# TensorE takes every other conditioning tile of the first quarter, with the raw tile standing and the vector's column moving

## What is computed

```python
cond = jax.nn.silu(c)                     # (1, 2048)
mod = cond @ w_ada[l] + b_ada[l]          # w_ada: 2048 x (9 * 2048) f32
sh1, sc1, gt1, sh2, sc2, gt2, sh3, sc3, gt3 = jnp.split(mod, N_MOD, axis=-1)
h = modulate(rmsnorm(x, g_ffn1_pre[l]), sh1, sc1)     # h * (1 + sc1) + sh1
y = rmsnorm(swiglu(h, w1_gate[l], w1_up[l], w1_down[l]), g_ffn1_post[l])
```

## Time and profile before

| | us |
|---|---|
| median of 3 runs (lowest, highest) | 1944.65 (1941.50, 1946.92) |
| the profiled execution | 1944.92 |
| its span, first to last instruction | 1943.1 |
| PE busy | 1862.8 (96%) |
| DVE busy | 1364.9 (70%) |
| ACT busy | 896.8 (46%) |

### The profile page before, as it was taken

The page is one execution under the profiler, slowest core; times in us unless marked ns, Lnnn a source line. Parts: engine busy times, 40 slices in busy tenths (PEclk is TensorE's granted clock), DMA queues, the critical chain, the costliest instruction groups (busy, mean ns, idle before and its releaser), DMA issues.

```text
span 1943.1 us, 24172 instructions
## 1 busy us (share of the span) xinstructions
PE 1862.8 (96%) x8522; PEld 1530.4 (79%) x8522; DVE 1364.9 (70%) x1667; ACT 896.8 (46%) x1138; POOL 0.2 (0%) x4
## 2 busy tenths in 40 slices
PE   3999999999999999799999997999999999999998
PEld 3788888888877778587887786888888888788886
DVE  6986877777778878879886796877654545544444
ACT  4677644444434433544445546444444444434443
POOL 0000000000000000000000000000000000000000
PEclk9999999999999999899999998999999999999999
DMA  9996888888878988678993494888766666566663
GB/s 372 391 385 215 268 273 270 282 289 278 287 263 309 359 298 306 226 248 283 306 307 115 137 335 136 274 288 279 251 190 189 190 188 192 167 193 195 194 195 131
DMA packets 254926, 488.26 MB, mean 251 GB/s; under 512 B 17414, under 2 KB 19836, under 8 KB 254588
## 3 DMA queue, kind: packets, MB, share of 16 engines
q1 hardware_dynamic: 253968, 486.66, 75.4%
q10 hardware_dynamic: 876, 0.53, 0.1%
HBM read 485.04 MB, written 2.10 MB: 251 GB/s over the span
## 4 chain that ended last, share of the span: by engine, by line
PE 83%; DVE 8%; DMA 3%; DVEq 3%; ACT 2%; issue 1%; SPq 0%; ACTq 0%
PE pair L1337 27%; PE pair L1339 26%; PE pair L1338 26%; DVE acc L856 2%; DMA raw<-in_w_down 2%; PE tps L1377 2%; DVE w_lo L837 2%; DVE start_acc L869 1%; DVEq L845 1%; DMA start_raw<-in_w_ada 1%; ACT w_hi L497 1%; PE mps L1421 1%; PE tps L1428 1%; PE mps L1404 0%; DVEq L868 0%
## 5 line engine op out<-in xcount | busy, mean ns | idle before, releaser
L497 ACT ACTIVATE w_hi<-raw 128x1024 fp32r<-128x1024 f32 x634 | 668.0, 1056 | 904.4 <-PE pair L1339 491.8
L837 DVE TENSOR_TENSOR w_lo<-raw,w_hi 128x1024 fp32r<-128x1024 f32 x634 | 769.8, 1218 | 427.0 <-ACT w_hi L497 423.2
L1337 PE MATMUL pair<-w_hi,h_hi 128*128 128x512 f32 (+1 forms) x1792 | 703.4, 393 | 10.2 <-DVE w_lo L837 8.8
L1339 PE MATMUL pair<-w_hi,h_lo 128*128 128x512 f32 (+1 forms) x1792 | 696.4, 389 | 0.0
L1338 PE MATMUL pair<-w_lo,h_hi 128*128 128x512 f32 (+1 forms) x1792 | 695.8, 388 | 0.0
L1337 PEld LDWEIGHTS pair<-w_hi,h_hi 128*128 128x128 f32 x1792 | 336.9, 188 | 83.6 <-DVE w_lo L837 6.9
L1339 PEld LDWEIGHTS pair<-w_hi,h_lo 128*128 128x128 f32 x1792 | 336.8, 188 | 69.9
L1338 PEld LDWEIGHTS pair<-w_lo,h_hi 128*128 128x128 f32 x1792 | 337.1, 188 | 66.8 <-issue 0.2
L856 DVE SCALAR_TENSOR_TENSOR acc<-raw,c_col,acc 128x512 f32<-128x512 f32 x420 | 315.6, 751 | 45.9 <-DMA raw<-in_w_ada 11.9
L1337 PE MATMUL pair<-w_hi,hid_hi 128*128 128x512 f32 x704 | 277.3, 394 | 5.7 <-DVE w_lo L837 5.7
L1339 PE MATMUL pair<-w_hi,hid_lo 128*128 128x512 f32 x704 | 274.3, 390 | 0.0
(11 more groups left out here) (161 smaller groups left out, 683.9 us busy)
## 6 DMA issues: line engine op xcount, KB each, us to landing
raw<-in_w_ada SPq DMA_DIRECT2D x224, 512.0 KB, 4.8
raw<-in_w_gate SPq DMA_DIRECT2D x176, 512.0 KB, 3.9
raw<-in_w_up SPq DMA_DIRECT2D x176, 512.0 KB, 4.1
raw<-in_w_down SPq DMA_DIRECT2D x176, 512.0 KB, 4.3
start_raw<-in_w_ada SPq DMA_DIRECT2D x64, 512.0 KB, 8.8
raw<-in_w_in SPq DMA_DIRECT2D x56, 512.0 KB, 4.6
raw<-in_w_o SPq DMA_DIRECT2D x32, 512.0 KB, 5.2
raw<-in_w_uq SPq DMA_DIRECT2D x6, 512.0 KB, 4.6
```

Of the source, the lines that this page charges most:

```text
L497: nc.scalar.activation(w_hi[:, w % HI_RING, :, 0:n], raw[:, r % RING, :, 0:n], ACT.Copy).then_inc(hi_ready, 1)
L837: nc.vector.tensor_tensor(w_lo[:, r % RING, :, 0:n], raw[:, r % RING, :, 0:n], w_hi[:, w % HI_RING, :, 0:n], ALU.subtract).then_inc(raw_us ...
L1337: nc.tensor.matmul(o, hi, wh, start=first and kk == 0, stop=False, skip_group_check=added)
L1339: ins = nc.tensor.matmul(o, lo, wh, start=False, stop=last and kk == 1, skip_group_check=added)
```

## The change

TensorE computes the products of the odd tiles of the first quarter (BY_PE) itself. start_turn(n) takes the raw tile as it landed: each of its 8 pieces of 128 columns is the standing operand, column j of silu(c) the moving one, and the products accumulate in the same 8 columns of mps into which start_columns(0) then adds the sums of VectorE's eight even tiles. start_turned counts these, and load_start waits for it where the tile whose buffer it reuses was TensorE's; start_used now counts VectorE's tiles only. On TensorE's queue tiles 1 and 3 stand ahead of the transposes of the columns, 5 to 11 behind them, both turns of x ahead of tile 13, then 13, 15 and start_columns(0). keep_warm(16) and the wait ahead of it are gone; keep_warm(20) stays. On VectorE the small works move to the places n = 6, 10 and 12. Later quarters are as before.

```diff
--- before.py
+++ after.py
@@ -60,6 +60,8 @@
 RING = 8
 HI_RING = 4
 START_RING = 7
+
+BY_PE = tuple(range(1, KD, 2))
 
 
 OPEN = 8
@@ -308,6 +310,7 @@
         restored = sem("restored")
         start_landed = [sem(f"start_landed{i}") for i in range(START_RING)]
         start_used = sem("start_used")
+        start_turned = sem("start_turned")
         start_sum = sem("start_sum")
         forget_landed = sem("forget_landed")
         rot_ready = sem("rot_ready")
@@ -362,6 +365,10 @@
                 if w < b.w_end:
                     return b, w - b.w
 
+        def by_dve(n):
+
+            return n - sum(k < n for k in BY_PE)
+
         def partial(v):
 
             return part[v % OPEN // OPEN_FF][:, v % OPEN_FF]
@@ -418,7 +425,11 @@
 
                 e, j = divmod(n, KD)
                 if n >= START_RING:
-                    sp.wait_ge(start_used, n - START_RING + 1)
+                    before = n - START_RING
+                    if before in BY_PE:
+                        sp.wait_ge(start_turned, BY_PE.index(before) + 1)
+                    else:
+                        sp.wait_ge(start_used, by_dve(before + 1))
                 sp.dma_start(start_raw[:, n % START_RING],
                              both[:, j, 0:2, e * NB:(e + 1) * NB]).then_inc(start_landed[n % START_RING], 16)
 
@@ -1053,11 +1064,13 @@
                 dve.wait_ge(setup, 1)
 
             for n in range(KD):
-                if n == 5:
+                if n in BY_PE:
+                    continue
+                if n == 6:
                     small_tiles()
-                if n == 9:
+                if n == 10:
                     power(N_X0, D, 2)
-                if n == 10:
+                if n == 12:
                     refine(N_X0)
                 start_ada(n)
 
@@ -1394,16 +1407,27 @@
                 for k in range(2):
                     transposes(n + k, [s[:, t, c * P:(c + 1) * P] for c in (2 * k, 2 * k + 1) for t in range(TT)], free)
 
+            def start_tile(tile, j, first, last):
+
+                for k in range(2 * DB):
+                    c = slice((k % 4) * P, (k % 4 + 1) * P)
+
+                    ins = nc.tensor.matmul(mps[:, 0, k:k + 1], tile[:, k // 4, c],
+                                           ones[:, 0:1] if j is None else c_col[:, 1, j:j + 1],
+                                           start=first and k == 0, stop=last, skip_group_check=True)
+                return ins
+
             def start_columns(e):
 
-                pe.wait_ge(start_used, KD * (e + 1))
+                pe.wait_ge(start_used, by_dve(KD * (e + 1)))
                 if e:
                     pe.wait_ge(gain_ready, e)
-                for k in range(2 * DB):
-                    c = slice((k % 4) * P, (k % 4 + 1) * P)
-                    ins = nc.tensor.matmul(mps[:, 0, k:k + 1], start_acc[:, e % 2, k // 4, c], ones[:, 0:1],
-                                           start=True, stop=True)
-                ins.then_inc(start_sum, 1)
+                start_tile(start_acc[:, e % 2], None, e > 0, True).then_inc(start_sum, 1)
+
+            def start_turn(n):
+
+                pe.wait_ge(start_landed[n % START_RING], 16 * (n // START_RING + 1))
+                start_tile(start_raw[:, n % START_RING], n, n == BY_PE[0], False).then_inc(start_turned, 1)
 
             def keep_warm(n):
 
@@ -1442,17 +1466,21 @@
                         after()
 
 
+            pe.wait_ge(c_ready, 1)
+            start_turn(1)
+            start_turn(3)
             pe.wait_ge(small_landed, SMALL)
             nc.tensor.transpose(mps[:, 1, 0:P], y[:, 0, 0:P], ident)
             rest = V_ROWS - P
             nc.tensor.transpose(mps[:, 1, P:V_ROWS], y[0:rest, 0, P:2 * P], cst[0:rest, 0:rest]).then_inc(cols_full, 1)
-            turn_x(tp["mod1"], XN["ffn1"], 0)
+            for n in BY_PE[2:]:
+                if n == 13:
+                    turn_x(tp["mod1"], XN["ffn1"], 0)
+                    turn_x(tp["mod1"], XN["ffn1"], 1)
+                start_turn(n)
+            start_columns(0)
 
             pe.wait_ge(setup, 1)
-            pe.wait_ge(start_used, KD - 3)
-            keep_warm(16)
-            start_columns(0)
-            turn_x(tp["mod1"], XN["ffn1"], 1)
             keep_warm(20)
 
             for v in range(4 * OPEN):
```

## The result

The changed kernel is slower: a median of 1951.81 us (9 runs, 1949.57 to 1953.75) against 1944.0 (9 runs, 1939.42 to 1948.83), a ratio of 1.0040 with an interval of 1.0032 to 1.0049, which is 7.8 us (6.2 to 9.5). Its profiled span is 1950.4 us, 7.3 more than before.

What follows compares the result with a forecast made beforehand. TensorE, busy 96%, bounds the kernel; what counts is when start_columns(0) ends: 38.76 becomes 44.9 (+6.1), taken as +6.4 on 1944.92, giving 1951.3, or 1951.0 for the median. Range 1945.5 to 1955.

Steps and rivals of the forecast that it cites:

- The price of a tile: TensorE's 16 one-column instructions per odd tile: 3.44 us at the low clock, against 2.57 us for two arrivals.
- The timetable: TensorE's opening: tiles 5 to 11 done at 32.7, turns 34.4, tiles 13 and 15 41.3, columns' end 44.9: +6.1 us.
- the waits ahead of the groups: Possible waits before TensorE's seven groups: 3.58 instead of 3.44 us each would make +7.1; +6.4 was taken.
- the mark: Not a forecast term: start of the second start_columns, at 80.64 in the kernel before, used to compare traces.
- The early part: Tiles 1 and 3 and column transposes on TensorE until about 14.5, hidden before 18.9; uncovered, it would cost 0.5 us.
- The clock: TensorE's opening: one-column matmuls don't lift the low 1.2 GHz clock, so groups stay at 3.44 us.
- rival A: Clock rises early under unbroken TensorE work, later tiles take 1.7 us: -3.5 us, 1941.2; chance 0.12.
- rival B: Clock rises at the turns of x; tiles 13, 15 and the columns take 1.7 us: +1.2 us, 1945.9; chance 0.06.
- Rival C: First weight products start at the low clock, +2.4 us after slack: +8.8 us in all, 1953.7; chance 0.12.
- Transfers: SyncE's queue: arrivals up to tile 15 hold despite later slot release; costed at nothing, at most 0.5 us for tile 14.
- What was removed: VectorE loses 8 of 16 passes, 11.0 us, and is no longer the bound; TensorE loses 16 idle-fill transposes, 3.65 us.
- From the start to the end: After 66.90 TensorE is busy without a gap for 60 us, so the opening's shift stays to the end.

Runs made afterwards that it cites:

- vector_stands: Changed kernel with operands exchanged: the vector's column stands, the raw tile moves in 512-column matmuls; tile 15 back on VectorE. Ratio to the kernel before 1.0009.
- fill_between: Changed kernel plus 16 identity transposes ahead of tile 5 and 8 behind each of tiles 5, 7 and 9. Ratio to the kernel before 1.0056.
- fill_wide: Changed kernel plus 512-column identity matmuls: 3 ahead of tile 5, one behind each of tiles 5, 7, 9 and 11. Ratio to the kernel before 1.0062.
- one_piece: Changed kernel with only 1 of 8 pieces of each odd tile computed on TensorE, queues and waits kept. Median 1943.17 us, ratio to the kernel before 0.9992.
- two_tiles: Changed kernel with only tiles 8 and 11 on TensorE, no fill ahead of the first columns. Ratio to the kernel before 0.9994.
- before_wide: Kernel before, all 16 tiles on VectorE, with 512-column matmuls (4, then 3) as fill instead of 16 transposes. Ratio to the kernel before 0.9999.
- rows_mid: Changed kernel with vector standing and tile moving, only tiles 5, 7, 9, 11 on TensorE, 3 wide matmuls ahead. Median 1941.68 us, ratio to before 0.9986.

## Why the prediction was right

**The price of a tile.** Forecast 3.44 us at the low clock, taken from L1404. Measured: tiles 5 to 11 start at 19.02 and the turns at 32.69, 3.42 each; tiles 13 and 15, from 34.43 to 41.12, 3.35 each.

**The timetable.** Forecast 32.7, 34.4, 41.3 and an end at 44.9 (+6.1), of which I took +6.4 for the waits ahead of the groups. Measured 32.69, 34.43, 41.12, 44.67 (+5.9). The waits cost nothing, as the row at 38.62 in the earlier trace rows had shown; the 0.3 I added for them was wrong. That the mark's 6.3 still meets the forecast's 6.4 is luck: the 0.5 us of idle VectorE at 66.87, which no step of mine had, made good for it. The first PE-bound stretch was forecast for 73.3 and begins at 73.24.

**The early part.** VectorE's copy to col was forecast for 14.7 and came at 15.60, as tile 3 reached TensorE only at 11.47; its next tile starts at 20.41, so the cover held. VectorE was forecast to be idle in 24 to 44; it works on its tiles until 31.9 and is idle from there to 44.71.

**The clock.** The inference that one-column matmuls don't lift it was the weakest step, from one stretch of 3.58 us. 25.7 us without a gap, all of it such matmuls but for 8 transposes, now bear it out, and rival A is refuted by the stretch 18.90 to 44.70. The Trainium skill, "TensorE: Matmul & The Clock Gate", "Why this matters for your kernels", advises to keep the engine continuously busy to reach the full clock; this stretch, at 0.21 us an instruction to its end, shows that continuous work alone is not enough. In vector_stands, where the tile moves, the clock rose. What I had not asked is whether such matmuls also let the clock fall; fill_between and fill_wide show that they do. Against rival B, the 8 transposes at 32.69 changed nothing: tiles 13 and 15 stayed slow. Rival C came close and was covered as said: the first weight product, at 48.69, still took 0.62 us, the next 0.39, and the mark is not later for it.

**The other rule.** That transpose mode doesn't engage the full clock (the Trainium skill, "TensorE: Matmul & The Clock Gate", part 4) is again not borne out: 30 transposes of which the first went at 0.22 us took 4.33 us in all, and the columns behind them ran at 1.95.

**Transfers.** Tile 14 was forecast to land at 30.5 and VectorE starts it at 30.63. TensorE waits for no tile after tile 5. The transfers then stand nearly still in 45 to 52 (86 GB/s), where the kernel before, whose queue waits in the same place of its order, keeps 402 GB/s in 39 to 46. The queue's wait ends at 51.2, forecast for about 51.7. As forecast, nothing is lost by it up to the mark: VectorE's start on the second quarter (50.90 for 44.98) is late by the same 5.9 us as the columns.

**What was removed.** VectorE's relief was real and worth nothing here: 12.79 us of waiting in its place. That its backlog was only 3.3 us behind the landings set the most that could be gained; one_piece, with TensorE's part nearly gone, gets 2.5 of them.

**From the start to the end.** The prediction let the shift stay to the end because TensorE is busy for 60 us behind 66.90. That holds up to the fourth start_columns, at 180. Behind it the shift is not constant (3.1 us at 1089.66, 4.6 at 1094.06, 7.3 at the end of the same trace), so this step did not carry what was put on it. In the twelve profiled runs beside before's the shift of the span differs from that of the mark by 0.3 us (fill_wide, two_tiles) up to 5.4 (fill_between), and before_wide has its mark 0.9 early and its span 1.4 longer. All are held against one trace of before, so its own course is in each of these differences. What carries the reading is the medians: they differ by 6.7 and 7.8, for a mark late by 6.1 and 6.3, and by 8.6 for the 8.8 of one_piece. Marks of 1 to 3 us are below what a single trace can promise for the time. The forecast median was 1951.0, the measured one 1951.81; the forecast lay just above what can be told from no change, and so does the result, with 1.0032 as the lower end of the first interval and 1.0020 as that of the second.

## What to carry to other kernels

An idle engine is worth what its own pace allows between two arrivals, not what it takes off the other: a tile took TensorE 3.4 us where two arrive in 2.6, so its idle time held two tiles and eight made a new bound. Before handing matrix-times-vector work to TensorE ask which operand moves: with the vector standing and the tile moving the same product ran at 1.88 us instead of 3.42. And matmuls that stand alone behind a wait on the path may run at the low clock: 30 transposes ahead of them, in time that was idle anyway, made 16 of them 1.6 us shorter, though the time of the whole kernel did not move clear of the noise.

## What the runs showed of the hardware

That one-column matmuls bring a raised clock down while TensorE is busy without a gap was new to me: in fill_between it is at 0.50 from 21.5 on, behind one group of 16 and 8 transposes, and in fill_wide it falls inside the third group. The transposes and the wide matmuls, which move 128 and 512 columns over a standing 128x128, do lift it. The kernels that raise the clock in the opening spread from 4.3 us (rows_mid) to 9.2 (fill_wide) over their runs; the kernel before, which raises it only at 42.8, spreads by 8.8 in the second round and the changed one by 4.2, so the spread doesn't follow from that. Only profiled runs show the clock.
